# Handing Pool's loads of value quads and of reread weights to ScalarE and SP in a hybrid decoder step

## The chip, the cores and the metric

The kernel runs on one core of one Trainium2 chip. The metric is the device time of one execution in microseconds (us). The median of three runs of the kernel before is 2049.36 us (2048.97 to 2071.32). Differences under 2% (about 41 us) are called no change here.

## The reference

Two decoder layers run for a prompt group (512 tokens) and a sample group (8 tokens, one from each of 8 sequences with 4096 past tokens). Both groups share all weights. Layer 0 mixes retention with differential attention; layer 1 is a gated MLP over chunks of 128 tokens. A squared-ReLU MLP follows each layer. Cut to what matters here:

```
proj = h @ w_in                                   # layer 0, both groups
k_past = cache_k[e][page_table]; v_past = cache_v[e][page_table]   # 8 sequences x 32 pages of 128 rows
a = softmax(q1 k1) - lam * softmax(q2 k2);  do = a @ v_all          # per sequence and head
mix = concat(retention, do) @ w_out
y = y + mix;  y = y + square(relu(rms_norm(y) @ w_up)) @ w_down      # both groups
z = gelu(rms_norm(y) @ w_in_odd); u, v = split(z); ...               # layer 1
```

## The kernel before, in words

All matrix products of the prompt are made from weight chunks of 512 x 256 elements (512 KB). SP loads a chunk into one of two `raw` buffers (L637). ScalarE makes its rounded part `w_hi` (L587), and VectorE the remainder `w_lo` (L594). PE multiplies three times for each pair of parts. The chunks of the dense part of layer 0 and of the v half of layer 1 form a list of 100 places, `DENSE`, which are called steps 0 to 99 below: output projection `oe` (0 to 11), the first half of the MLP `up00` (12 to 27) and `dn00` (28 to 43), its second half `up01` (44 to 59) and `dn01` (60 to 75), and `v` (76 to 99). Each engine walks through this list in the same order, and does after its own part of a step whatever `AFTER[step]` lists for it.

Two kinds of work of the samples are listed there. `("V", i)` is the product of value quad i with the attention weights: four pages of the value cache, 1 MB, 64 quads in all, of which 30 are used up before the dense part. `("W", n)` is the product of the samples' few columns with a quad of weights (512 x 512, again 1 MB), 50 in all, in steps 47 to 89. These weights are read a second time from HBM, in other blocks than SP's chunks. There are five `W` to four steps, so eleven steps hold two. Both kinds go through the same two buffers, `vbuf0` and `vbuf1`: quad u may be loaded when quad u-2 has been used (`v_used`). PE does the product of a quad at the end of the step, after the step's chunk.

In the kernel before Pool issues all these loads (`quad_in`): at its place `("V", i)` it loads quad i+1, and at `("W", n)` quad n+1 of the weights. For a value page it reads the page's number into a register first. In the same program order Pool has other work: per macro (two chunks) of `up00` and `up01` the squares and remainders of the MLP's middle (L832, L814), sums of squares in `oe` and `dn01` (L800), the maximum over partitions for a sequence's softmax (L775), and the loads for the gating (L839 to L843). ScalarE's rounding of the middle (L1214) stands between Pool's L832 and L814.

SP's program order is, per step i: load chunk i+5, then the pages of keys listed there. What holds the load of a chunk is

```
wait(sp, lo_made, c.n - 1)                 # SP, chunk c = 41 + i: the remainder of step i+3 is made
wait(act, chunk_multiplied, c.n - 3)       # ScalarE, L587: step i+3 is rounded once step i-1 is multiplied
```

So SP's load at its step i leaves after PE has finished the chunk of step i-1, ScalarE has rounded and VectorE has made the remainder of another chunk. In `v` a macro's two chunks are multiplied together, four token tiles in turn; the first chunk counts as multiplied only with the last tile, and `AFTER` of the macro's two steps stands after the second and the fourth tile.

Of the kernel before, what the change touches and what calls it, by code (L numbers as in the profile page):

```python
# [26 lines left out]
P = 128  # L27
# [28 lines left out]
def _phases():  # L56
# [24 lines left out]
QUAD = 4  # L81
NQ, SQ = NG // QUAD, NPAGES // QUAD
K_SLOTS, Q_SLOTS = 4, 2
# [3 lines left out]
W_BLOCKS = [("oe", c, 3) for c in range(2)] + [("up", c, 2) for c in range(8)] + [("dn", c, 8) for c in range(2)] + [  # L87
    ("vv", c, 2) for c in range(6)]
W_QUADS = [(b, g) for b, (_, _, n) in enumerate(W_BLOCKS) for g in range(n)]
NW = len(W_QUADS)  # L90
# [135 lines left out]
NV1 = sum(s[0] == "V" for s in FIRST)  # L226
# [38 lines left out]
def wait(eng, sem, value):  # L265

    if isinstance(value, int) and value <= 0:
        return
    eng.wait_ge(sem, value)
# [50 lines left out]
def build(nc, x_prompt, x_sample, state_ret, cache_k, cache_v, page_table, rms_mix_g, rms_ffn_g, w_ffn_up, w_ffn_down,  # L320
# [3 lines left out]
    with ExitStack() as ctx:  # L324
# [119 lines left out]
        def kbuf(j):  # L444

            slot = j % K_SLOTS
            return kbuf_low[slot] if slot < LOW_KEYS else (kbuf_in_x if j < K1 else kbuf_on)[slot - LOW_KEYS]

        def vbuf(n):

            return vbuf_low if n % Q_SLOTS == 0 else vbuf_in_x if n < NV1 else vbuf_on
# [64 lines left out]
        def sem(name):  # L516
            return ctx.enter_context(nc.semaphore(name))
# [17 lines left out]
            sem(n) for n in ("turn_ready", "turn_read", "out_ready", "out_read", "pair_ready"))  # L535
        k_loaded = [sem(f"k_loaded{i}") for i in range(K_SLOTS)]
        v_loaded = [sem(f"v_loaded{i}") for i in range(Q_SLOTS)]
        k_scored, v_used = sem("k_scored"), sem("v_used")
        pv_zeroed, z_summed = sem("pv_zeroed"), sem("z_summed")
        k_weighed = sem("k_weighed")  # L540
# [21 lines left out]
        so_turned, so_placed, f_placed = sem("so_turned"), sem("so_placed"), sem("f_placed")  # L562
# [26 lines left out]
        def lo(dve, c):  # L589

            if isinstance(c.n, int) and c.n >= CHUNKS:
                return
            dve.wait_ge(hi_made, c.n + 1)
            dve.tensor_tensor(w_lo[:, c.slot], raw[:, c.slot % 2], w_hi[:, c.slot].bitcast(F32),  # L594
                              ALU.subtract).then_inc(lo_made, 1)
# [6 lines left out]
        def page(eng, dst, cache, n, done):  # L602

            pg = eng.value_load(ptb[0:1, n:n + 1])
            eng.dma_start(dst, cache[0][bass.ds(pg, 1)].rearrange("a t h d -> (a t) (h d)")).then_inc(done, 16)  # L605

        def osb(i):

            return osb1 if i < 1 else osb2
# [3 lines left out]
            W_OF[f"up0{h}"] = w_ffn_up[0][:, 2048 * h:2048 * h + 2048]  # L613
            W_OF[f"dn0{h}"] = w_ffn_down[0][2048 * h:2048 * h + 2048, :]
        S_OF = {"oe": (w_out_even[0], mTs), "up": (w_ffn_up[0], xgs), "dn": (w_ffn_down[0], hs), "vv": (w_in_odd[0][:, E_G:2 * E_G], xgs)}

        def quad_landed(n):

            return 16 * QUAD * (min(n, NQ) // 2 + (1 if n < NQ else 0)) + (0 if n < NQ else 16 * ((n - NQ) // 2 + 1))

        block = ctx.enter_context(nc.Block())

# [2 lines left out]
        def _(sp):  # L625
# [13 lines left out]
            def keys_in(j):  # L639
                if j < NP:  # L640
                    wait(sp, k_scored, j - K_SLOTS + 1)
                    for a in range(PER):
                        page(sp, kbuf(j)[:, a, :], cache_k, PER * j + a, k_loaded[j % K_SLOTS])

            def in_chunk(c):

                if c < 2 * N_IN:
                    chunk_in(Chunk(0, 0, 0, c), w_in_even[0], c % 2, IN_COLS[c // 2])
                elif c < PHASES["u0"][0]:
                    name, m, g = DENSE[c - 2 * N_IN]  # L650
                    chunk_in(Chunk(0, 0, 0, c), W_OF[name], g, CW * m)
# [21 lines left out]
            for m in range(N_IN + 1):  # L673
                for t in range(NT + 1):
# [12 lines left out]
                    for step in AFTER[m, t]:  # L687
# [8 lines left out]
                        if step[0] == "K" and step[1] > 0:  # L696
                            j = step[1] - 1 + K_SLOTS
# [3 lines left out]
            for j in range(K1, K1 + K_SLOTS - 1):  # L701
                if j % K_SLOTS >= LOW_KEYS:
                    keys_in(j)
            for i, key in enumerate(DENSE):
                in_chunk(2 * N_IN + AHEAD + 2 + i)
                for step in AFTER[key]:
                    if step[0] == "K":
                        keys_in(step[1] - 1 + K_SLOTS)

            def stream(name, w, per):  # L710
                c0, groups, macros = PHASES[name]

                def step(i):
                    for mm in range(per):
                        for g in range(groups):
                            chunk_in(Chunk(c0, groups * per, i, groups * mm + g), w, g, CW * per * i + CW * mm)
                repeat(sp, macros // per, step, first=1)
# [22 lines left out]
        def _(pool):  # L740
# [10 lines left out]
            pool.wait_ge(lo_made, AHEAD)  # L751
            pool.wait_ge(pt_loaded, 16)
            pool.wait_ge(xg_lo_made, KD)
            def quad_in(u):

                if u < NQ + NW:
                    wait(pool, v_used, u - Q_SLOTS + 1)
                    dst, done = vbuf(u), v_loaded[u % Q_SLOTS]
                    if u >= NV1 and u % Q_SLOTS:
                        pool.wait_ge(so_turned, 1)  # L760
                    if u < NQ:
                        for j in range(QUAD):
                            page(pool, dst[:, j, :], cache_v, QUAD * u + j, done)
                    else:
                        b, g = W_QUADS[u - NQ]
                        phase, c, _ = W_BLOCKS[b]
                        rows = S_OF[phase][0].rearrange("(g k p) n -> g p k n", k=QUAD, p=P)[g]
                        pool.dma_start(dst[:, :, :], rows[:, :, 512 * c:512 * c + 512]).then_inc(done, 16)

            def pool_steps(key):  # L770

                for kind, i, *_ in [s + (0,) for s in AFTER[key]]:
                    if kind == "soft1":
                        pool.wait_ge(row_max, i + 1)
                        pool.partition_all_reduce(mxa, mx8, P, bass.bass_isa.ReduceOp.max).then_inc(all_max, 1)  # L775
                    elif kind == "V" and i > 0:
                        quad_in(i - 1 + Q_SLOTS)
                    elif kind == "W":
                        quad_in(NQ + i - 1 + Q_SLOTS)
            for m in range(N_IN + 1):  # L780
                for t in range(NT + 1):
                    if m < LO_SWITCH and t == 1:
                        lo(pool, Chunk(0, 0, 0, 2 * m + AHEAD))
                    pool_steps((m, t))
                if m < LO_SWITCH:
                    lo(pool, Chunk(0, 0, 0, 2 * m + 1 + AHEAD))
                if 2 <= m < 2 + Q_SLOTS:
                    pool.wait_ge(x_saved, 16)
                    quad_in(m - 2)

            def add_square(e, n):

# [85 lines left out]
        def _(act):  # L878
            chain = Chain(act, act_chain)

            for row, v in ((0, rms_mix_g), (16, rms_ffn_g), (32, ln_v_g), (56, ln_v_b), (80, subln_g)):
                n = int(np.prod(v.shape)) // P
# [88 lines left out]
            def act_step(step):  # L971
                kind, i = step[0], step[1] if len(step) > 1 else None
                if kind == "ropeq":
                    n = ROPED.index(i)
# [3 lines left out]
                elif kind == "ropet":  # L978
                    n = ROPED.index(i)
# [9 lines left out]
                elif kind == "turn":  # L989
                    hh = step[2]  # L990
                    act.wait_ge(turn_ready, TURN_FILL[step] + 1)
                    dst = {0: qT, 2: kT, 6: rqT, 8: rkT}[i & ~1][:, 2 * (i % 2) + hh, :]
# [21 lines left out]
                elif kind == "softe":  # L1014
# [2 lines left out]
                    wait(act, z_summed, i - 1)  # L1017
                    act.activation(Pe[:, i % 2], Sc[:, i % 2, 0:NPAGES, :], ACT.Exp, scale=SCALE)
                    act.activation(pn[:, 8 * i:8 * i + 8], Sc[:, i % 2, NPAGES, :], ACT.Exp, scale=SCALE).then_inc(exped, 1)
                elif kind == "pvO":  # L1020
                    act.wait_ge(v_used, QUADS_TO[i])
                    if i:
# [5 lines left out]
                elif kind == "pvT" and W_BLOCKS[i - NS][0] == "vv":  # L1028
                    c = W_BLOCKS[i - NS][1]
# [81 lines left out]
                elif kind == "rB":  # L1111
                    h, n = step[1:]
# [4 lines left out]
                elif kind == "rC":  # L1117
                    h, n = step[1:]
# [108 lines left out]
            c0, _, macros = PHASES["v"]  # L1227
# [547 lines left out]
        def _(pe):  # L1775
# [67 lines left out]
            def pe_step(step):  # L1843
                kind, i = step[0], step[1] if len(step) > 1 else None
                if step in TURN_FILL:
                    wait(pe, turn_read, TURN_FILL[step])
                if kind == "turn":
                    n, hh = ROPED.index(i), step[2]
# [13 lines left out]
                elif kind == "V":  # L1862
                    s, n = i // SQ, i % SQ
                    if n == 0:
                        pe.wait_ge(exped, s + 1)
                        wait(pe, o_copied, s - 1)
                    pe.wait_ge(v_loaded[i % Q_SLOTS], quad_landed(i))
                    for j in range(QUAD):
                        at = P // QUAD * j
                        last = pe.matmul(ps[at:at + 8, PV[s % 2], :], Pe[:, s % 2, QUAD * n + j, :], vbuf(i)[:, j, :],  # L1870
# [2 lines left out]
                elif kind == "W":  # L1873
                    b, g = W_QUADS[i]
                    phase, c, groups = W_BLOCKS[b]
# [7 lines left out]
                    else:  # L1883
                        pe.wait_ge(xgs_made, 1 if phase == "up" else 2)
                    u = NQ + i
                    pe.wait_ge(v_loaded[u % Q_SLOTS], quad_landed(u))
                    for j in range(QUAD):
                        at = P // QUAD * j
                        last = pe.matmul(ps[at:at + NS, PV[b % 2], :], S_OF[phase][1][:, QUAD * g + j, :], vbuf(u)[:, j, :],  # L1889
# [2 lines left out]
                elif kind == "pvT":  # L1892
# [3 lines left out]
                    for h in range(H):  # L1896
                        last = pe.matmul(ps[:, OUT, w * h:w * h + w], osb(i)[:, P * h:P * h + P],
                                         C["fold"][:, 2 * h:2 * h + 2] if i < NS else C["fold"], start=True, stop=True)
# [74 lines left out]
                elif kind == "dA":  # L1973
# [5 lines left out]
                    for m in range(2):  # L1979
                        rows, out = slice(DH * m, DH * m + DH), ps[:, PAIR[m], 0:nk]  # L1980
# [19 lines left out]
                elif kind == "rA":  # L2000
                    h, n = step[1:]
                    c = NT * h + n
# [12 lines left out]
                elif kind == "rB":  # L2015
                    h, n = step[1:]
                    c = NT * h + n
# [115 lines left out]
            c0, _, macros = PHASES["v"]  # L2133
# [85 lines left out]
```

## Time and profile before

| | |
|---|---|
| median of 3 runs | 2049.36 us |
| time of the profiled execution | 2051.19 us |
| its span, first to last instruction | 2049.5 us |
| PE busy | 1833.3 us (89%) |
| VectorE, ScalarE, Pool busy | 1011.3, 597.1, 459.5 us |
| mean granted TensorE clock | 0.938 |
| moved by DMA | 340.31 MB, of it 120.87 MB on Pool's queue |

The profile is of one execution. A busy engine is not necessarily the bound: idle time before a group of instructions and what ended it tell more. `SPq` and `POOLq` rows are DMA issues and register work of an engine's queue. The clock is granted in two levels, full (2.4 GHz) and half (1.2 GHz).

### The profile page before, as it was taken

How to read it: one execution, taken by the hardware profiler on the slowest of the kernel's cores; microseconds unless marked ns; L12 is line 12 of the kernel's file. 1: busy time of each engine (PE TensorE's matmuls, PEld its weight loads, DVE VectorE, ACT ScalarE, POOL GpSimd, SP SyncE). 2: the span in 40 equal slices, each digit the busy share in tenths (PEclk: the TensorE clock that was granted, in tenths of full speed). 3: DMA queues.
4: the chain of work that ended last, by engine and by line, in shares of the span. 5: the costliest groups of instructions: out<-in, count | busy, mean ns of one | idle time of the engine just before them, and what ended most of it. 6: DMA issues, size and time to landing. Idle time of an engine off the chain costs nothing.

```text
span 2049.5 us, 31901 instructions
## 1 busy us (share of the span) xinstructions
PE 1833.3 (89%) x12483; PEld 1538.4 (75%) x12483; DVE 1011.3 (49%) x1344; ACT 597.1 (29%) x962; POOL 459.5 (22%) x567
## 2 busy tenths in 40 slices
PE   6858888899688878999869899989999999999998
PEld 5656546676465555677646578989999999999998
DVE  3897656887777667323213233344323443323321
ACT  5322223444323122112212133363313333212221
POOL 1321011222023444214322111003304224102400
PEclk9977778999799889999989999999999999999999
DMA  5556344798888568645556756412323232323321
GB/s 144 166 175 227 113 137 141 249 314 302 272 282 287 185 237 280 220 164 195 168 180 207 248 193 218 134 54 63 103 93 93 83 99 87 101 88 89 94 93 63
DMA packets 215634, 340.31 MB, mean 166 GB/s; under 512 B 13793, under 2 KB 150706, under 8 KB 215234
## 3 DMA queue, kind: packets, MB, share of 16 engines
q1 hardware_dynamic: 178432, 214.75, 32.3%
q0 software_dynamic: 34704, 120.87, 17.8%
q10 hardware_dynamic: 2362, 2.83, 0.4%
q8 instruction: 90, 1.47, 0.3%
q14 instruction: 46, 0.38, 0.1%
HBM read 327.19 MB, written 11.21 MB: 165 GB/s over the span
## 4 chain that ended last, share of the span: by engine, by line
PE 64%; issue 14%; DVE 8%; DMA 5%; POOL 4%; ACT 4%; POOLq 1%; ACTq 0%; SPq 0%; DVEq 0%
PE ps L2095 10%; PE ps L2093 10%; PE ps L2094 10%; PE ps L1835 5%; PE ps L1837 4%; PE ps L1836 4%; PE ps L2082 3%; PE ps L2084 3%; PE ps L2083 3%; PE ps L1870 2%; PE ps L1981 2%; PE ps L1889 2%; DMA vbuf<-in_cache_v 1%; DVE Sc L1425 1%; POOL tmp L832 1%
## 5 line engine op out<-in xcount | busy, mean ns | idle before, releaser
L594 DVE TENSOR_TENSOR w_lo<-raw,w_hi 128x1024 fp32r<-128x1024 f32 x238 | 327.5, 1381 | 482.6 <-ACT w_hi L587 481.2
L587 ACT ACTIVATE w_hi<-raw 128x1024 fp32r<-128x1024 f32 x248 | 259.2, 1053 | 410.6 <-PE ps L2095 228.1
L1835 PE MATMUL ps<-w_hi,xg_hi 128*128 128x256 f32 x960 | 290.7, 303 | 9.6 <-ACT part L916 3.2
L1836 PE MATMUL ps<-w_lo,xg_hi 128*128 128x256 f32 x960 | 279.3, 291 | 0.0
L1837 PE MATMUL ps<-w_hi,xg_lo 128*128 128x256 f32 x960 | 278.7, 290 | 0.0
L2093 PE MATMUL ps<-xg_hi,w_hi 128*128 128x260 f32 x896 | 253.2, 283 | 0.8 <-DVE vn L1761 0.8
L2095 PE MATMUL ps<-xg_hi,w_lo 128*128 128x260 f32 x896 | 253.1, 283 | 0.0
L2094 PE MATMUL ps<-xg_lo,w_hi 128*128 128x260 f32 x896 | 252.3, 282 | 0.0
L1835 PEld LDWEIGHTS ps<-w_hi,xg_hi 128*128 128x128 f32 x960 | 192.2, 200 | 49.2 <-issue 36.1
L1836 PEld LDWEIGHTS ps<-w_lo,xg_hi 128*128 128x128 f32 x960 | 192.1, 200 | 0.2
L1837 PEld LDWEIGHTS ps<-w_hi,xg_lo 128*128 128x128 f32 x960 | 191.3, 199 | 0.0
L2093 PEld LDWEIGHTS ps<-xg_hi,w_hi 128*128 128x128 f32 x896 | 168.6, 188 | 1.1 <-DVE vn L1761 1.0
L2095 PEld LDWEIGHTS ps<-xg_hi,w_lo 128*128 128x128 f32 x896 | 168.6, 188 | 0.0
L2094 PEld LDWEIGHTS ps<-xg_lo,w_hi 128*128 128x128 f32 x896 | 168.5, 188 | 0.0
L605 POOL DMA_DIRECT2D vbuf<-in_cache_v x196 | 107.2, 548 | 263.3 <-PE ps L1870 144.5
L2093 PE MATMUL ps<-h_hi,w_hi 128*128 128x260 f32 x512 | 144.6, 282 | 0.0
L2095 PE MATMUL ps<-h_hi,w_lo 128*128 128x260 f32 x512 | 144.6, 282 | 0.0
L2094 PE MATMUL ps<-h_lo,w_hi 128*128 128x260 f32 x512 | 144.5, 282 | 0.0
L832 POOL TENSOR_TENSOR tmp<-tmp 128x512 f32<-128x512 f32 (+1 forms) x64 | 65.7, 1047 | 292.3 <-DVE tmp L1700 285.3
L1422 DVE TENSOR_TENSOR kbuf<-kbuf,Qb 128x1024 f32<-128x1024 f32 x88 | 109.0, 1239 | 6.6 <-DMA kbuf<-in_cache_k 3.5
L1425 DVE TENSOR_REDUCE Sc<-kbuf 128x16 f32<-128x1024 f32 x88 | 107.4, 1220 | 3.0
L2095 PE MATMUL ps<-g_hi,w_lo 128*128 128x260 f32 x384 | 108.8, 283 | 0.0
(348 smaller groups left out, 3573.0 us busy)
## 6 DMA issues: line engine op xcount, KB each, us to landing
vbuf<-in_cache_v POOLq DMA_DIRECT2D x196, 256.0 KB, 4.6
kbuf<-in_cache_k SPq DMA_DIRECT2D x176, 256.0 KB, 4.8
raw<-in_w_ffn_up SPq DMA_DIRECT2D x64, 512.0 KB, 4.1
raw<-in_w_ffn_down SPq DMA_DIRECT2D x64, 512.0 KB, 4.1
raw<-in_w_in_odd SPq DMA_DIRECT2D x48, 512.0 KB, 3.8
raw<-in_w_in_even SPq DMA_DIRECT2D x36, 512.0 KB, 5.1
vbuf<-in_w_ffn_up POOLq DMA_DIRECT2D x16, 1024.0 KB, 6.0
vbuf<-in_w_ffn_down POOLq DMA_DIRECT2D x16, 1024.0 KB, 5.6
```

The source lines that it names most:

```text
L587: act.activation(w_hi[:, c.slot], raw[:, c.slot % 2], ACT.Copy).then_inc(hi_made, 1)
L594: dve.tensor_tensor(w_lo[:, c.slot], raw[:, c.slot % 2], w_hi[:, c.slot].bitcast(F32), ALU.subtract).then_inc(lo_made, 1)
L605: eng.dma_start(dst, cache[0][bass.ds(pg, 1)].rearrange("a t h d -> (a t) (h d)")).then_inc(done, 16)
L832: pool.tensor_tensor(tmp2[:, b, 0:w], tmp1[:, b, 0:w], tmp1[:, b, 0:w], ALU.mult).then_inc(mid_made, 1)
L1422: dve.tensor_tensor(kk[:, :, :], kk[:, :, :], Qb[:, s % 2, :].unsqueeze(1).broadcast_to([P, PER, 512]), ALU.mult).then_inc(k_weighed, 1)
L1425: dve.tensor_reduce(Sc[:, s % 2, g:g + PER, :], kk[:, :, :].rearrange("p a (b c) -> p a b c", c=DH), AXX, ALU.add).then_inc(k_scored, 1)
L1835: pe.matmul(out, xh, wh, start=kk == 0, stop=False, skip_group_check=True)
L1836: pe.matmul(out, xh, wl, start=False, stop=False, skip_group_check=True)
L1837: mm = pe.matmul(out, xl, wh, start=False, stop=kk == KD - 1, skip_group_check=True)
L2093: pe.matmul(out, wh, xh, start=kk == 0, stop=False, skip_group_check=True)
L2094: pe.matmul(out, wh, xl, start=False, stop=False, skip_group_check=True)
L2095: mm_ = pe.matmul(out, wl, xh, start=False, stop=kk == KC * groups - 1, skip_group_check=True)
```

## The change

The loads of reread weights go from Pool to SP: after its chunk of a step, SP issues at `("V", 63)` quad 0 and at `("W", n)` quad n+1. Value quads 0 to 30 and the even ones after that stay with Pool; the 17 odd ones from 31 to 63 are issued by ScalarE, at the same places of the list, on a semaphore of their own. Products, buffers and the list itself stay. In the diff `sample_weights_in` is SP's and the last `values_in(act, ...)` ScalarE's.

```
+        def by_pool(u):
+            return u <= NV1 or u < NQ and u % Q_SLOTS == 0
+        def quad_landed(u):
+            if by_pool(u):
+                return v_loaded[u % Q_SLOTS], 16 * QUAD * (u // Q_SLOTS + 1)
+            return v_loaded_on[u % Q_SLOTS], sum(16 * (QUAD if n < NQ else 1) for n in range(u, 0, -Q_SLOTS) if not by_pool(n))
+        def values_in(eng, u):
+            if u < NQ:
+                wait(eng, v_used, u - Q_SLOTS + 1)
+                if u >= NV1 and u % Q_SLOTS:
+                    eng.wait_ge(so_turned, 1)
+                for j in range(QUAD):
+                    page(eng, vbuf(u)[:, j, :], cache_v, QUAD * u + j, quad_landed(u)[0])
...
+            def sample_weights_in(n):
+                u = NQ + n
+                sp.wait_ge(v_used, u - Q_SLOTS + 1)
...
+                sp.dma_start(vbuf(u)[:, :, :], rows[:, :, 512 * c:512 * c + 512]).then_inc(quad_landed(u)[0], 16)
             for i, key in enumerate(DENSE):
                 in_chunk(2 * N_IN + AHEAD + 2 + i)
                 for step in AFTER[key]:
                     if step[0] == "K":
                         keys_in(step[1] - 1 + K_SLOTS)
+                    if step == ("V", NQ - 1):
+                        sample_weights_in(0)
+                    if step[0] == "W" and step[1] + 1 < NW:
+                        sample_weights_in(step[1] + 1)
...
-                    elif kind == "V" and i > 0:
-                        quad_in(i - 1 + Q_SLOTS)
-                    elif kind == "W":
-                        quad_in(NQ + i - 1 + Q_SLOTS)
+                    elif kind == "V" and i > 0 and by_pool(i - 1 + Q_SLOTS):
+                        values_in(pool, i - 1 + Q_SLOTS)
...
+                elif kind == "V" and i > 0 and not by_pool(i - 1 + Q_SLOTS):
+                    values_in(act, i - 1 + Q_SLOTS)
...
-                    pe.wait_ge(v_loaded[u % Q_SLOTS], quad_landed(u))
+                    pe.wait_ge(*quad_landed(u))
```

What the change moves shows at two places. The first is Pool in macros 0 to 4 of `v` (`vbuf_71` is `vbuf0`, `vbuf_115` is `vbuf1`): before, the weights' loads stand there one behind the other, and nothing but `v_used` holds them (`so_turned` was reached long before).

```order
885 L768 DMA vbuf_71<-in_w_ffn_down 128x4x512 [waits v_used]
886 L768 DMA vbuf_115<-in_w_ffn_down 128x4x512 [waits so_turned,v_used]
887 L768 DMA vbuf_71<-in_w_in_odd 128x4x512 [waits v_used]
888 L768 DMA vbuf_115<-in_w_in_odd 128x4x512 [waits so_turned,v_used]
889 L768 DMA vbuf_71<-in_w_in_odd 128x4x512 [waits v_used]
890 L768 DMA vbuf_115<-in_w_in_odd 128x4x512 [waits so_turned,v_used]
```

The same loads now stand on SP, from quad 37 of the weights (first row) to quad 42 (last but one):

```order
912 L726 DMA vbuf_115<-in_w_ffn_down 128x4x512 [waits v_used]
913 L726 DMA vbuf_71<-in_w_in_odd 128x4x512 [waits v_used]
914 L652 DMA raw<-in_w_in_odd 128x4x256 [waits lo_made] x3
915 L726 DMA vbuf_115<-in_w_in_odd 128x4x512 [waits v_used]
916 L726 DMA vbuf_71<-in_w_in_odd 128x4x512 [waits v_used]
917 L652 DMA raw<-in_w_in_odd 128x4x256 [waits lo_made]
918 L726 DMA vbuf_115<-in_w_in_odd 128x4x512 [waits v_used]
919 L652 DMA raw<-in_w_in_odd 128x4x256 [waits lo_made]
920 L726 DMA vbuf_71<-in_w_in_odd 128x4x512 [waits v_used]
```

Quad 39 (row 915) moved from a place behind quad 38 alone to one behind three chunks that wait for `lo_made`.

The second place is Pool at the end of `oe`, before: quad 39 of the values (rows 500 to 511) stands behind the maximum over partitions.

```order
498 L775 ISA
499 L775 ISA tiny<-tiny 128x8 [waits row_max]
500 L604 TENSOR_LOAD ptb [waits so_turned,v_used]
501 L605 ISA
502 L605 DMA vbuf_115<-in_cache_v 128x512
```

The same quad now stands on ScalarE, behind the rounding of a chunk:

```order
456 L588 ACTIVATE w_hi<-raw 128x1024 [waits raw_loaded0,chunk_multiplied]
457 L588 ACTIVATE w_hi<-raw 128x1024 [waits raw_loaded1,chunk_multiplied]
458 L605 TENSOR_LOAD ptb [waits so_turned,v_used]
459 L606 ISA
460 L606 DMA vbuf_115<-in_cache_v 128x512
```

It no longer follows row 499; the next `w_hi` of ScalarE now follows its four pages.

## Rows read from the trace of the kernel before

**Rows 1.** Groups by line, PE's sample products: busy, mean ns | idle before, releaser.
```profile
L1870 PE MATMUL ps<-vbuf,Pe 128*8 128x512 f32 x392 | 56.0, 646 | 37.0 <-DMA vbuf<-in_cache_v 37.0
L1889 PE MATMUL ps<-vbuf,xgs 128*8 128x512 f32 x224 | 32.4, 656 | 26.2 <-DMA vbuf<-in_w_ffn_up 25.7 <-DMA vbuf<-in_w_in_odd 0.5
L1889 PE MATMUL ps<-vbuf,hs 128*8 128x512 f32 x128 | 16.5, 594 | 7.6 <-DMA vbuf<-in_w_ffn_down 7.6
```

**Rows 2.** Timeline of PE, value quads 39, 42, 47: start, duration, [idle before <-releaser].
```profile
660.76 1.89 PE L1870 MATMUL ps<-vbuf,Pe 128*8 128x512 f32 x8 [6.21 <-DMA vbuf<-in_cache_v]
...
701.90 1.90 PE L1870 MATMUL ps<-vbuf,Pe 128*8 128x512 f32 x8 [6.34 <-DMA vbuf<-in_cache_v]
...
759.72 1.90 PE L1870 MATMUL ps<-vbuf,Pe 128*8 128x512 f32 x8 [13.52 <-DMA vbuf<-in_cache_v]
```

**Rows 3.** Timeline of Pool around the loads of value quads 39, 42 and 47.
```profile
652.68 0.40 POOL L775 PARTITION_ALL_REDUCE tiny<-tiny  x1 [10.61 <-issue]
...
670.30 2.66 POOL L800 TENSOR_TENSOR sqsum<-sqsum,sq 128x512 f32<-128x512 f32 x2 [8.68 <-issue]
...
751.43 1.83 POOL L605 DMA_DIRECT2D vbuf<-in_cache_v  x3
```

**Rows 4.** Timeline of ScalarE, the two chunks rounded before value quad 47.
```profile
749.58 1.99 ACT L587 ACTIVATE w_hi<-raw 128x1024 fp32r<-128x1024 f32 x2
```

**Rows 5.** Timeline of SP, issue of four pages of keys.
```profile
717.31 3.07 SPq L605 DMA_DIRECT2D kbuf<-in_cache_k  x4
```

**Rows 6.** Timeline of PE, reread weights: quads 7, 15, 32, 36+37, 38+39, 48+49.
```profile
992.44 1.89 PE L1889 MATMUL ps<-vbuf,xgs 128*8 128x512 f32 x8 [5.41 <-DMA vbuf<-in_w_ffn_up]
...
1066.39 1.90 PE L1889 MATMUL ps<-vbuf,xgs 128*8 128x512 f32 x8 [15.17 <-DMA vbuf<-in_w_ffn_up]
...
1176.18 1.04 PE L1889 MATMUL ps<-vbuf,hs 128*8 128x512 f32 x8 [2.92 <-DMA vbuf<-in_w_ffn_down]
...
1212.29 1.90 PE L1889 MATMUL ps<-vbuf,hs 128*8 128x512 f32 x16
...
1234.30 1.90 PE L1889 MATMUL ps<-vbuf,xgs 128*8 128x512 f32 x16
...
1295.43 2.09 PE L1889 MATMUL ps<-vbuf,xgs 128*8 128x512 f32 x16
```

**Rows 7.** Timeline of SP, loads of chunks at steps 54, 74, 77+78, 81, 89.
```profile
987.47 0.37 SPq L637 DMA_DIRECT2D raw<-in_w_ffn_up  x1
...
1167.20 0.37 SPq L637 DMA_DIRECT2D raw<-in_w_in_odd  x1
...
1207.42 2.70 SPq L637 DMA_DIRECT2D raw<-in_w_in_odd  x2
...
1237.11 0.37 SPq L637 DMA_DIRECT2D raw<-in_w_in_odd  x1
...
1297.46 0.37 SPq L637 DMA_DIRECT2D raw<-in_w_in_odd  x1
```

**Rows 8.** DMA issues: queue, count, KB each, median us from issue to landing.
```profile
vbuf<-in_cache_v POOLq DMA_DIRECT2D x196, 256.0 KB, 4.6
kbuf<-in_cache_k SPq DMA_DIRECT2D x176, 256.0 KB, 4.8
raw<-in_w_ffn_up SPq DMA_DIRECT2D x64, 512.0 KB, 4.1
...
vbuf<-in_w_ffn_up POOLq DMA_DIRECT2D x16, 1024.0 KB, 6.0
vbuf<-in_w_ffn_down POOLq DMA_DIRECT2D x16, 1024.0 KB, 5.6
...
xT<-x_kept SPq DMA_DIRECT2D x1, 2080.0 KB, 7.9
```

**Rows 9.** Waits: who waited for whom, us in total, times, longest.
```profile
POOL vbuf L768 <- issue: 187.6, 37, 7.3
```

**Rows 10.** Windows: stretch, length, busy of PE to POOL, PEclk, DMA share, GB/s.
```profile
760.00:770.00 10.00, 10.00 (x41) 5.89 (x34) 6.80 (x7) 3.74 (x5) 7.21 (x9) 0.75 0.82 296
```

More of the change, by code:

```diff
@@ L537, in build @@
         v_loaded = [sem(f"v_loaded{i}") for i in range(Q_SLOTS)]
+        v_loaded_on = [sem(f"v_loaded_on{i}") for i in range(Q_SLOTS)]
         k_scored, v_used = sem("k_scored"), sem("v_used")
@@ L615, in build @@
         S_OF = {"oe": (w_out_even[0], mTs), "up": (w_ffn_up[0], xgs), "dn": (w_ffn_down[0], hs), "vv": (w_in_odd[0][:, E_G:2 * E_G], xgs)}
-        def quad_landed(n):
-            return 16 * QUAD * (min(n, NQ) // 2 + (1 if n < NQ else 0)) + (0 if n < NQ else 16 * ((n - NQ) // 2 + 1))
         block = ctx.enter_context(nc.Block())
@@ L703, in _ @@
                     keys_in(j)
+            def sample_weights_in(n):
+                u = NQ + n
+                sp.wait_ge(v_used, u - Q_SLOTS + 1)
+                b, g = W_QUADS[n]
+                phase, c, _ = W_BLOCKS[b]
+                rows = S_OF[phase][0].rearrange("(g k p) n -> g p k n", k=QUAD, p=P)[g]
+                sp.dma_start(vbuf(u)[:, :, :], rows[:, :, 512 * c:512 * c + 512]).then_inc(quad_landed(u)[0], 16)
             for i, key in enumerate(DENSE):
@@ L753, in _ @@
             pool.wait_ge(xg_lo_made, KD)
[L754 to L768, printed above, removed]
             def pool_steps(key):
@@ L788, in _ @@
                     pool.wait_ge(x_saved, 16)
-                    quad_in(m - 2)
+                    values_in(pool, m - 2)
             def add_square(e, n):
@@ L1866, in pe_step @@
                         wait(pe, o_copied, s - 1)
-                    pe.wait_ge(v_loaded[i % Q_SLOTS], quad_landed(i))
+                    pe.wait_ge(*quad_landed(i))
                     for j in range(QUAD):
```

## Prediction

> **What bounds the kernel now.** Read the groups by line first. PE is busy for 89% of the span, so only what makes PE wait or slows its clock can move the end. Two of PE's groups are touched: the samples' value products (L1870), which wait 37.0 us in all for value loads, and their products with reread weights (L1889), which wait 26.2 + 7.6 = 33.8 us [rows 1]. That is the stock from which the change could gain: about 71 us, 3.5% of the span. PE's timeline then tells where the stock lies. Three value quads hold 26 of the 37 us: 39 with 6.2, 42 with 6.3 and 47 with 13.5 us [rows 2]. Of the weights, quad 15 alone holds 15.2 us; the rest is a few us at the second product of a double step, such as 5.4 at quad 7 and 2.9 at quad 32, all of it in `up01` and `dn01` [rows 6]. In `v` PE goes through both products of a step without a wait: 36 and 37, 38 and 39, 48 and 49 each stand as one row of 16 matmuls [rows 6].
>
> Each long wait has a second price. In the ten us behind the wait of 13.5 us the granted clock is 0.75 [rows 10], part of the time at the half level of 1.2 GHz: 2.5 us lost. The eight products behind waits of 5.4 and 15.2 us take 1.89 us instead of 1.04, those behind 2.9 us don't [rows 6]. I charge 2.5 us for a wait of five us or more, 1.5 for the one of 3.9 at quad 12, nothing below three.
>
> **The weights on SP.** What holds such a load changes. On Pool it was `v_used` and Pool's queue; on SP it also stands behind the chunk load of its step, which leaves only when a remainder is made, that is after PE has finished the chunk before. For a double step (quads n, n+1) the load of n+1 stands behind this step's chunk, and PE wants it at the end of this step. So I take the time of SP's chunk load, add what the load takes, and compare with the time at which PE came to the product.
>
> The price of a 1 MB load on SP isn't in the trace. The nearest rows are Pool's own 1 MB loads, 6.0 and 5.6 us [rows 8]; I take 5.8, plus 0.9 for the two issues (0.37 for the chunk [rows 7], about as much for the quad): the quad lands 6.7 us after the chunk load began. The ends are SP's 512 KB chunk, 4.1 us, and SP's 2080 KB load, 7.9 us [rows 8]; 5.8 is nearest because size and pattern are the same and only the issuer differs.
>
> The Trainium skill ("DMA: Bandwidth & Descriptors", "Issuing engine by pattern") calls issue from SP or ScalarE generally faster than from Pool, with a first byte after about 0.6 instead of 1 us. By it each of 14 late loads would be 0.4 us earlier, some 6 us less in the sum (an estimate); this trace doesn't show it, as SP's 256 KB pages land after 4.8 us and Pool's after 4.6 [rows 8].
>
> *up01 and dn01*, seven doubles. Quad 7: chunk load at 987.5 [rows 7] + 6.7 = 994.2; PE was ready at 992.4 − 5.4 = 987.0 [rows 6]: a wait of 7.1 us, against 5.4. Quad 32: 1167.2 + 6.7 = 1173.9 against 1173.3: 0.6, against 2.9. Worked out alike the seven give 3.1 (quad 2), 7.1, 5.8, 3.0, 0.7, 1.4 and 0.6 = 21.7 us, against 17.7 now. Quad 15's wait of 15.2 goes: it comes from the gating's loads ahead of it on Pool (L839 to L843), which SP doesn't have; so does 0.8 of quad 28. Sum 21.7 − 33.7 = **−12.0**.
>
> *v*, four doubles and the singles around them. Here the load of the chunk at a macro's second step leaves only when the macro's last tile is multiplied, which is when PE turns to the samples. Quad 39: 1237.1 + 6.7 = 1243.8, wanted at 1234.3 + 1.0 = 1235.3 [rows 6, 7]: 8.5 us of wait where there was none. Quad 44 has the same place (8.5); quad 49: 1297.5 + 6.7 − 1296.4 = 7.8. Quads 36 and 37 stand behind the two chunk loads at 1207.4 and 1209.8: 1214.1 against 1212.3, then 1216.5 against 1215.1, so 1.8 and 1.4. Quads 42 and 47, each 1.9. Sum 31.8, against 0.5 now: **+31.3**.
>
> *Clock.* Slowed stretches now: behind quads 7, 15 (2.5 each) and 12 (1.5) = 6.5; then: behind 7, 12, 39, 44, 49 = 12.5. **+6**.
>
> SP's wait for `v_used` is satisfied no later than the next chunk's own condition, so I cost nothing for chunks behind it; they are loaded five steps ahead. If that cover were gone, ScalarE's rounding would be late next.
>
> **The values.** Quad 39's load stood on Pool behind the maximum over partitions, with 10.6 us of idle time charged to "issue" before it and 8.7 more before the sums behind it [rows 3]. On ScalarE it leaves at once, so its 6.2 us go; but PE next waits for Pool's sums of squares (L800), which come some 4 to 5 us earlier because Pool has shed this quad's issue: of 6.2 I count **−5**, without a clock gain. Quad 47 leaves Pool at 751.4 [rows 3]; on ScalarE it stands behind the rounding of a chunk, done at about 750.6 [rows 4]: **−0.8**. Quad 42, with the even 34, 36, 38, 50 and 52, stays on Pool. Its DMA now meets that of ScalarE's quad beside it: two loads share the engines, where 1 MB more costs (7.9 − 4.1) / 1568 KB = 2.5 us [rows 8]; I charge 1.5 each at 42 and 52: **+3**. ScalarE issues 17 quads at the 3.07 us that SP needs for four pages [rows 5], 52 us in all; ScalarE works three steps ahead of PE, which hides one issue per step, so 0; without that cover the next `w_hi`, and PE behind it, would be up to 3 us late, 17 times. Pool's saved 2.3 us or so per quad free idle Pool time, 0.
>
> **The sum:** −12.0 + 31.3 + 6 − 2.8 = +22.5 us. The sum is against the profiled execution (2051.2), which is 1.8 above the median of the runs; on the median, 2049.4 + 22.5 = **2072 us**. With loads of 4.1 us instead of 5.8 the fourteen waits shrink and two fall under the clock's price: about +1, 2051. With 7.9 us: about +51, 2100.
>
> **The rivals.**
>
> *A, the forecast:* late weights in `v` cost more than quad 15 gives: 2055 to 2090. Chance 0.58.
>
> *B, the values win.* If the "issue" time before Pool's work [rows 3, 9] is its queue being full, half the pages on another engine could empty it: nearly all 37.0 us at L1870 [rows 1] and four slowed stretches of 2.3 go, 46 us; less 25 for the weights: about 2028. For it: Pool's quad loads wait 187.6 us for "issue", 37 times [rows 9]; against it, the largest waits, 42 and 47, stay behind the same macro's work. Chance 0.11; 2% faster (2008) needs the weights to come free as well.
>
> *C, slower.* One mechanism: 1 MB through SP's queue lands later than Pool's, behind the 512 KB chunk issued just ahead of it on the same queue. At 7.2 us or more, 1.4 later on 14 waits, 20 us more: 2092, and 2100 at the far end of 7.9 [rows 8]. It decides from 7.2 us. For it: the chunk is still moving when the quad starts, and 1 MB costs 2.5 us by the slope above; against it, Pool's 5.8 already held such neighbours. Chance 0.18.
>
> *D, no difference.* The loads are the same bytes on the same DMA engines; if the issuer only spends its own time, PE's waits stay about what they are: 2049. This is against the order of instructions, by which a load in `v` can't leave before the chunk load, and against the 187.6 us that Pool's loads waited at issue [rows 9]. Chance 0.09.
> The Trainium skill says so in "DMA: Bandwidth & Descriptors", "Issuing engines are not separate DMA queues": spreading issues over engines parallelises only the issuing, usually a small gain. This trace disagrees as far as rows 9 go: here the issuing engine's queue held loads back.
>
> The remaining 0.04 is for what I haven't seen, such as ScalarE losing its cover.
>
> **Range and chances.** A, D and half of C lie between 2045 and 2097, about 0.8. Faster by over 2% (2008): 0.03; slower by over 2% (2090): C and the tail of A, 0.19; within: 0.78. Two per cent, 41 us, is about what a measurement of this kernel can tell from no change, given runs from 2049.0 to 2071.3.
>
> **What the profile would show.** Right: PE idle about 8 us before the second product of quads 39, 44 and 49, none at quad 15, and quad 39 of the values without a wait; DMA issues of 1 MB on SP near 5.8 us; waits at value quads 42, 47 and 52 much as before. Wrong: SP's quads landing before PE's second product in `v`; waits at 42 and 47 gone (B); or new idle time before L587 or before PE's first product of a chunk, which would mean that ScalarE's or SP's lead doesn't hide the new issues.

## The result, and the profile after

The changed kernel takes 2097.03 us (median of 4 runs, 2096.78 to 2102.31). The kernel before, in runs on the same chips, takes 2055.72 (2048.97 to 2071.32). The ratio is 1.0196, 95% interval 1.0129 to 1.0264: slower by 27 to 54 us. That it is slower is clear of the scatter; whether by more than the 2% line is not, since the interval lies on both sides of it. The profiled execution took 2102.31 us with a span of 2100.6, 51.1 longer than the profiled one of before. PE is busy for 1845.7 us instead of 1833.3 with the same 12483 instructions, and the mean granted clock is 0.928 instead of 0.938.

The groups by line of the changed kernel, PE's sample products and its products with Pool's sums (busy, mean ns | idle before, releaser; to be held against [rows 1]):

```profile
L1882 PE MATMUL ps<-vbuf,Pe 128*8 128x512 f32 x392 | 55.3, 638 | 41.0 <-DMA vbuf<-in_cache_v 41.0
L1901 PE MATMUL ps<-vbuf,xgs 128*8 128x512 f32 x224 | 35.0, 702 | 45.0 <-DMA vbuf<-in_w_in_odd 27.1 <-DMA vbuf<-in_w_ffn_up 17.9
L1901 PE MATMUL ps<-vbuf,hs 128*8 128x512 f32 x128 | 18.7, 659 | 11.8 <-DMA vbuf<-in_w_ffn_down 11.8
L1901 PE MATMUL ps<-vbuf,mTs 128*8 128x512 f32 x48 | 7.1, 668 | 6.7 <-DMA vbuf<-in_w_out_even 6.7
L2133 PE MATMUL ps<-sqsum,ones 128*128 128x512 f32 x4 | 3.2, 888 | 6.8 <-POOL sqsum L810 6.8
```

Before, the last two of these groups read:

```profile
L1889 PE MATMUL ps<-vbuf,mTs 128*8 128x512 f32 x48 | 6.3, 594 | 0.3 <-DMA vbuf<-in_w_out_even 0.3
L2121 PE MATMUL ps<-sqsum,ones 128*128 128x512 f32 x4 | 3.2, 886 | 3.1 <-POOL sqsum L800 3.1
```

Waits for reread weights rose from 34.1 to 63.5 us; the largest part, 27.1, is in `v`, where there was 0.5. Value waits rose from 37.0 to 41.0, and the wait for Pool's sums of squares from 3.1 to 6.8. With 12.4 us more of PE's busy time that is 49.5 of the 51.1 us.

This sum runs over the whole span, and part of the span is not touched by the change. The next two views cut both executions at the same products of PE: at the ends of value quad 29 (all loads up to here are as before), value quad 63, reread quad 35 (`up01` and `dn01`) and reread quad 49 (`v`). The columns are the stretch, its length, PE's busy time, the granted clock, the share of the DMA engines and GB/s. Before:

```profile
0.00:529.40 529.40, 429.03 (x2806) 0.87 0.60 197
529.40:903.10 373.70, 314.45 (x1481) 0.91 0.73 251
903.10:1205.70 302.60, 264.29 (x1313) 0.94 0.58 190
1205.70:1297.50 91.80, 91.31 (x763) 1.00 0.66 218
1297.50:2049.50 752.00, 734.19 (x6131) 0.99 0.28 86
```

After:

```profile
0.00:523.40 523.40, 421.50 (x2806) 0.88 0.61 198
523.40:907.30 383.90, 316.83 (x1477) 0.90 0.73 245
907.30:1213.30 306.00, 269.55 (x1317) 0.93 0.54 185
1213.30:1345.70 132.40, 100.75 (x767) 0.87 0.46 163
1345.70:2100.60 754.90, 737.13 (x6128) 0.99 0.28 85
```

The first stretch is 6.0 us shorter after; over the eleven profiled kernels, none of which changes anything there, it takes 517.6 to 529.4 us, so this is scatter. Behind it the changed execution is 57 us longer: 10.2 in the values, 3.4 in `up01` and `dn01`, 40.6 in `v`, 2.9 in the rest. PE's busy time behind the first stretch rose by some 20 us, not 12.4; 9.4 of them are in `v`, where the granted clock fell from 1.00 to 0.87.

PE's timeline of the changed kernel (start, duration, what ended the idle time): value quads 39, 47 and 50, then reread quads 15, 32, 37, 39, 44 and 49.

```profile
660.24 1.05 PE L1882 MATMUL ps<-vbuf,Pe 128*8 128x512 f32 x8
...
759.61 1.89 PE L1882 MATMUL ps<-vbuf,Pe 128*8 128x512 f32 x8 [12.04 <-DMA vbuf<-in_cache_v]
...
800.33 1.90 PE L1882 MATMUL ps<-vbuf,Pe 128*8 128x512 f32 x8 [12.53 <-DMA vbuf<-in_cache_v]
...
1068.90 1.04 PE L1901 MATMUL ps<-vbuf,xgs 128*8 128x512 f32 x8 [0.56 <-DMA vbuf<-in_w_ffn_up]
...
1179.84 1.89 PE L1901 MATMUL ps<-vbuf,hs 128*8 128x512 f32 x8 [2.69 <-DMA vbuf<-in_w_ffn_down]
...
1225.65 1.89 PE L1901 MATMUL ps<-vbuf,hs 128*8 128x512 f32 x8 [3.07 <-DMA vbuf<-in_w_ffn_down]
...
1258.31 1.89 PE L1901 MATMUL ps<-vbuf,xgs 128*8 128x512 f32 x8 [8.36 <-DMA vbuf<-in_w_in_odd]
...
1302.21 1.90 PE L1901 MATMUL ps<-vbuf,xgs 128*8 128x512 f32 x8 [8.09 <-DMA vbuf<-in_w_in_odd]
...
1343.80 1.89 PE L1901 MATMUL ps<-vbuf,xgs 128*8 128x512 f32 x8 [7.51 <-DMA vbuf<-in_w_in_odd]
```

Value quad 39 no longer waits, quad 47 waits 12.0 us in place of 13.5 [rows 2], and quad 50, an even one that stayed on Pool, waits 12.5; before, quad 50 waited 1.4 and quad 52 5.9, which is gone. Reread quad 15 has lost its 15.2 us, and quads 39, 44 and 49 have waits of about 8 us where there were none [rows 6].

SP's timeline around reread quad 39's load shows the mechanism: the chunk load of step 81, and behind it quad 39 (with quad 40).

```profile
1251.71 0.37 SPq L652 DMA_DIRECT2D raw<-in_w_in_odd  x1
1252.12 1.06 SPq L726 DMA_DIRECT2D vbuf<-in_w_in_odd  x2
```

PE had finished the macro and came to quad 39 at about 1250; the product starts 6.6 us after the chunk load.

### The profile page after: what moved, and what is told of

Read it like the earlier page. It is cut to its first block, busy times and chain, and to the rows that moved or that the text cites. A ratio compares the mean times of both kernels' runs of the same rounds, so it can differ in the third digit from the quotient of the medians.

```text
span 2100.6 us, 31879 instructions
## 1 busy us (share of the span) xinstructions
PE 1845.7 (88%) x12483; PEld 1546.8 (74%) x12483; DVE 1011.5 (48%) x1344; ACT 596.7 (28%) x962; POOL 384.8 (18%) x449
## 4 chain that ended last, share of the span: by engine, by line
PE 61%; issue 15%; DVE 8%; DMA 7%; ACT 4%; POOL 3%; POOLq 1%; SPq 0%; ACTq 0%; DVEq 0%
PE ps L2107 10%; PE ps L2105 10%; PE ps L2106 10%; PE ps L1847 4%; PE ps L1849 4%; PE ps L1848 4%; PE ps L2094 3%; PE ps L2096 3%; PE ps L2095 2%; PE ps L1882 2%; PE ps L1993 2%; DMA vbuf<-in_w_ffn_down 1%; DMA vbuf<-in_w_in_odd 1%; POOL tmp L842 1%; PE ps L1901 1%
## 5 line engine op out<-in xcount | busy, mean ns | idle before, releaser
L1847 PE MATMUL ps<-w_hi,xg_hi 128*128 128x256 f32 x960 | 294.3, 307 | 9.1 <-DVE xg_lo L1682 3.1
L1847 PEld LDWEIGHTS ps<-w_hi,xg_hi 128*128 128x128 f32 x960 | 195.4, 204 | 52.8 <-issue 41.8
L606 POOL DMA_DIRECT2D vbuf<-in_cache_v x128 | 70.3, 550 | 248.6 <-PE ps L1882 124.5
```

Source lines behind the costliest of these rows:

```text
L1847: pe.matmul(out, xh, wh, start=kk == 0, stop=False, skip_group_check=True)
```

## The experiments

The theory after the result: the weights on SP cost the time, because they stand behind chunk loads that have no lead over PE. The rivals: ScalarE's value loads cost it, or SP's queue is slower for 1 MB. Each ratio is to runs of the kernel before on the same chip; those spread from 2042 to 2069 us over all the experiments, and the intervals allow for that. Medians of different experiments come from different chips; a difference of a few us between two of them is not sharp.

**One half of the change at a time.** All values on Pool, weights on SP (`e1`), by one line of `by_pool`:

```
-            return u <= NV1 or u < NQ and u % Q_SLOTS == 0
+            return u < NQ
```

> All values stay on Pool, only the reread weights go to SP. Theory (the weights cost the time, because SP's load of a weight quad leaves behind a chunk load that leaves only when PE is done with the chunk before): waits at L1901 of about 60 us in place of 34, 8 us each at quads 39, 44 and 49, none at 15; 2075 to 2090 us. Rival (ScalarE's value loads cost it, by colliding with Pool's): 2045 to 2055 us.

Measured: 2084.79 us, ratio 1.0162 (1.0135 to 1.0188). The waits at L1901 add up to 60.5 us (by the weights that are read: 6.0 for `oe`'s, 17.4 for `up01`'s, 8.9 for `dn01`'s, 28.3 for `v`'s), 8.5, 8.0 and 7.9 of them at quads 39, 44 and 49. The theory's figures hold.

The other half (`e2`): weights on Pool as before, odd values on ScalarE:

```
+            return u <= NV1 or u >= NQ or u % Q_SLOTS == 0
...
+                    elif kind == "W" and i + 1 < NW:
+                        sample_weights_in(i + 1)
```

> The reread weights stay on Pool, the odd values go to ScalarE. Theory: quad 39's wait is gone, quads 42 and 47 wait as before, a few us more at the even quads; reread weights wait 34 us as before; 2045 to 2058 us. Rival (ScalarE's loads cost the time): over 2070 us.

Measured: 2061.55 us, ratio 1.0043 (1.0019 to 1.0067): slower by 7 us by the medians and 9 by the ratio, under the 2% line but clear of the scatter, and a little above the times expected. Quad 39's wait is gone, but the value waits are 40.5 us in all: 5.0 at quad 36 and 11.6 at quad 50, and PE waits 9.0 us for Pool's sums of squares. The reread weights wait 37.7 us, a few more than expected. The two ratios multiply to 1.0206; the whole change has 1.0196. So the weights make some four fifths of the loss, the values the rest.

**The place behind the chunk load** (`e3`): the changed kernel, but with the first reread quad of a step issued ahead of the step's chunk.

```
+                first = next((step for step in AFTER[key] if step[0] == "W" and step[1] + 1 < NW), None)
+                if first:
+                    sample_weights_in(first[1] + 1)
                 in_chunk(2 * N_IN + AHEAD + 2 + i)
...
-                    if step[0] == "W" and step[1] + 1 < NW:
+                    if step[0] == "W" and step[1] + 1 < NW and step != first:
                         sample_weights_in(step[1] + 1)
```

> The changed kernel, but SP issues the first reread quad of a step ahead of the step's chunk load instead of behind it. Theory (what is late is the place behind the chunk load): waits at quads 39, 44 and 49 fall from 8 us each to under 2, the 1 MB loads land after about 5.8 us instead of 7.2, and the time comes to 2045 to 2062 us. Rival (SP's queue is simply slower for 1 MB than Pool's, wherever the load stands): they still take about 7 us to land, and the time stays over 2080 us.

Measured: 2018.17 us, ratio 0.9823 (0.9787 to 0.9859), better than expected. Its PE groups:

```profile
L1904 PE MATMUL ps<-vbuf,xgs 128*8 128x512 f32 x224 | 28.3, 594 | 3.4 <-DMA vbuf<-in_w_ffn_up 1.8 <-DMA vbuf<-in_w_in_odd 1.6
L1904 PE MATMUL ps<-vbuf,hs 128*8 128x512 f32 x128 | 16.5, 594 | 1.9 <-DMA vbuf<-in_w_ffn_down 1.9
L1904 PE MATMUL ps<-vbuf,mTs 128*8 128x512 f32 x48 | 6.3, 594 | 1.8 <-DMA vbuf<-in_w_out_even 1.8
```

Of 63.5 us 7.1 are left, and the mean of one product is 594 ns throughout, with no slowed ones. The same loads on the same queue, two lines earlier, turn a loss into a gain of 36 us for the kernel as a whole. This is the experiment that shows the cause. Cut into the same stretches, `e3` takes 263.4 us in `up01` and `dn01` (302.6 before, 306.0 in the changed kernel) and 93.9 us in `v` (91.8 and 132.4). So the new order takes away the loss in `v`; the gain over the kernel before is made in `up01` and `dn01`, for a reason that `e4` shows. By the Trainium skill ("DMA: Bandwidth & Descriptors", "Issuing engines are not separate DMA queues") issuing from several engines saves only the time of issuing, usually a small gain. Here the place in the issuer's order was worth 79 us by the medians (77 by the ratios) between two kernels that use the same engines.

**Where the loss is made** (`e7`): values on Pool, reread quads 0 to 37 on SP behind the chunks as in the change, 38 to 49 on Pool.

```
+            return u < NQ or u >= NQ + 38
...
+                    if step[0] == "W" and step[1] + 1 < 38:
+                        weights_in(sp, step[1] + 1)
...
+                    elif kind == "W" and 38 <= i + 1 < NW:
+                        weights_in(pool, i + 1)
```

> Values on Pool, reread weights 0 to 37 on SP behind the chunk loads as in the change, 38 to 49 on Pool again. Theory (nearly all of the loss is made in v, by quads 39, 44 and 49 and their clock): about 31 us less than the run with all weights on SP, 2050 to 2058 us, no wait over 2 us from quad 39 on. Rival (the loss is made in oe, up01 and dn01, where 1 MB loads take 7 us): 2070 us or more.

Measured: 2051.04 us, ratio 0.9973 (0.9948 to 0.9998), and no wait over 1.5 us from quad 39 on. The 12 quads of `v` cost the 34 us between this run and `e1` (39 by the ratios); the 38 before them are worth nothing or a few us of gain on SP.

**Quad 15** (`e4`): the kernel before, with Pool's gating loads moved behind its work in `dn01`.

```
-                if h:
-                    gate_in()
                 between(f"dn0{h}", 2 if h else None)
+            gate_in()
```

> The kernel before, with Pool's five loads for the gating moved behind its work in dn01. Theory (quad 15's wait of 15.2 us is these loads' time on Pool): that wait goes, with 2.5 us of slowed clock: about 2032 us. Rival (the wait comes from something else on Pool at the turn from up01 to dn01): quad 15 waits 10 us or more still, 2049 us.

Measured: 2052.17 us, ratio 0.9991 (0.9966 to 1.0017): no change. The wait at quad 15 is gone, as expected, and yet nothing is won: the waits for weights add up to 33.1 us, against 34.1 before. 5.2 of it stand at quad 35, where the gating's loads now are, those at quads 17 to 32 rose from 8.9 to 14.3 and those behind quad 35 from 0.5 to 4.0; quads 7 and 12 wait 9.5, against 9.3. Pool's timeline of this kernel, loads of weights with nothing else between them:

```profile
1151.32 0.76 POOL L768 DMA_DIRECT2D vbuf<-in_w_ffn_down  x1 [7.10 <-issue]
1157.49 0.76 POOL L768 DMA_DIRECT2D vbuf<-in_w_ffn_down  x1 [5.42 <-issue]
1163.14 0.75 POOL L768 DMA_DIRECT2D vbuf<-in_w_ffn_down  x1 [4.89 <-issue]
1169.36 0.76 POOL L768 DMA_DIRECT2D vbuf<-in_w_ffn_down  x1 [5.46 <-issue]
```

They leave 5.7 to 6.2 us apart, each held by "issue". What holds them shows in the landings: these four landed 5.9, 5.3, 5.9 and 5.3 us after they left, and each next one leaves 0.3 us after the one before it has landed. In the kernel before this holds for 37 of the 49 pairs of consecutive reread loads on Pool, and none leaves earlier, though `v_used` would let it. PE uses five quads in four steps of about 6.7 us and one more product, some 5.6 us a quad. So in `up01` and `dn01` Pool's own pace sets the time: a wait taken away at one quad comes back at the next ones. That explains the miss; it was read from the trace and not tried by itself. On SP, which issues two 1 MB loads in 1.06 us (rows above), the pace is not there: in the changed kernel 29 of the 49 leave before the one ahead has landed, and in `e3` the waits did go.

**Values back to Pool with the weights ahead** (`e5`): `e3` with the line of `e1`.

> As the run with the reread weights ahead of the chunk load, but with all values back on Pool. If the two halves of the change add up, as the two runs of one half each suggest (30.6 and 7.3 us), this is some 7 us faster than that run: about 2011 us, with value waits as in the kernel before (34 to 37 us). Rival (ScalarE's values cost nothing, and the 7 us are scatter): 2018 us.

Measured: 2009.08 us, ratio 0.9765 (0.9725 to 0.9806), 9 us under `e3`, though the intervals of the two ratios overlap. The traces agree on the size better: from value quad 29 to value quad 63 the split costs 7.5 us here (375.3 against 382.8 in `e3`), and some 12 both with the late weights (372.3 in `e1`, 383.9 in the changed kernel) and with the weights on Pool (373.7 before, 386.0 in `e2`). So the split of the values costs time with and without the late weights.

**All dense quads on SP** (`e6`): `by_pool` is `u <= NV1`, nothing is issued by ScalarE, and the first quad of a step, values or weights, goes ahead of the chunk.

```
+                quads = [u for u in quads if NV1 < u < NQ + NW]
+                for u in quads[:1]:
+                    reread_in(u)
                 in_chunk(2 * N_IN + AHEAD + 2 + i)
...
+                for u in quads[1:]:
+                    reread_in(u)
```

> All value quads of the dense part go to SP as well, and the first reread quad of a step, values or weights, is issued ahead of the step's chunk load. Theory (the value waits come from the place behind Pool's other work and from Pool's pauses between pages): the 35 to 40 us at the value products fall below 12 and the time to 1970 to 1995 us. Rival (the value waits are DMA time, with 270 GB/s moved in these stretches): they stay over 30 us, or the chunk loads behind them become late and PE waits at its first product of a chunk; 2010 us or more.

Measured: **1979.59 us**, ratio 0.9636 (0.9589 to 0.9683), faster than both kernels by 3.6% and 5.6%. Value waits fell to 19.3 us, not below 12 as expected, and 12.1 of these stand at quad 48; quad 47 (the first row), where the long wait was before, has 0.5:

```profile
717.28 1.04 PE L1889 MATMUL ps<-vbuf,Pe 128*8 128x512 f32 x8 [0.53 <-DMA vbuf<-in_cache_v]
...
736.20 1.89 PE L1889 MATMUL ps<-vbuf,Pe 128*8 128x512 f32 x8 [12.10 <-DMA vbuf<-in_cache_v]
```

Pool's timeline of `e6` ahead of that wait shows the maximum over partitions and the squares behind it; SP's, below it, shows a chunk load, which waits for a remainder, and quad 48 behind it.

```profile
710.64 0.40 POOL L796 PARTITION_ALL_REDUCE tiny<-tiny  x1 [10.39 <-DVE tiny L1569]
719.33 2.04 POOL L851 TENSOR_TENSOR tmp<-tmp 128x512 f32<-128x512 f32 x2 [8.29 <-issue]
```

```profile
725.00 0.39 SPq L652 DMA_DIRECT2D raw<-in_w_ffn_up  x1
...
729.45 3.15 SPq L606 DMA_DIRECT2D vbuf<-in_cache_v  x4
```

**The maximum behind the squares** (`e8`): `e6` with Pool's squares of a macro ahead of the maximum.

```
-                                pool_steps((name, 2 * i + mm, g))
+                                pool_steps((name, 2 * i + mm, g), ("V",))
                         for b in range(2):
                             make(b, 4 * i + 2 * mm + b)
+                        if name in L0:
+                            for g in range(2):
+                                pool_steps((name, 2 * i + mm, g), ("soft1",))
```

> As the run with all dense quads on SP, but in up00 and up01 Pool does the squares of a macro ahead of the maximum over partitions listed there. Theory (the 12 us at quad 47, which stay whoever issues the load, come from this maximum: Pool's squares stand 8.3 us behind it, ScalarE's rounding of the middle waits for them, the next chunk's rounding for that, and SP's load of quad 47 for the chunk's remainder): the wait at quad 47 falls below 6 us and the time by 6 to 10 us, to 1970 to 1974 us. Rival (the wait comes from the DMA engines or the load's own place): 10 us or more stay, and the time stays at 1980 us.

The wait that this calls quad 47's is quad 48's in `e6`, as shown above.

Measured: 1981.40 us, ratio 0.9629 (0.9602 to 0.9656), the same as `e6`. Its PE and Pool timelines:

```profile
735.29 1.90 PE L1892 MATMUL ps<-vbuf,Pe 128*8 128x512 f32 x8 [4.37 <-DMA vbuf<-in_cache_v]
...
769.75 1.90 PE L1892 MATMUL ps<-vbuf,Pe 128*8 128x512 f32 x8 [4.46 <-DMA vbuf<-in_cache_v]
```

```profile
719.22 1.04 POOL L854 TENSOR_TENSOR tmp<-tmp 128x512 f32<-128x512 f32 x1
726.99 0.39 POOL L796 PARTITION_ALL_REDUCE tiny<-tiny  x1 [6.73 <-issue]
735.20 2.52 POOL L836 TENSOR_TENSOR hA_lo<-tmp,hA_hi 128x512 fp32r<-128x512 f32 x2 [7.81 <-issue]
```

The wait at quad 48 fell from 12.1 to 4.4 us, so most of it came from the maximum's place ahead of the squares; in the other kernels, where quad 47 waits, this was not tried. The median did not follow. Between 720.3 and 735.2 Pool's only row is the maximum, of 0.4 us, with idle time charged to "issue" before and behind it; it now stands ahead of the next remainders and squares, and the wait at quad 51 rose from 2.4 to 4.5. From value quad 29 to value quad 63 the profiled execution is 2.7 us shorter than that of `e6` (346.1 against 348.8), and the untouched stretch before it 6.6 us longer, so the runs cannot tell whether a few us were won.

**All dense values on ScalarE** (`e9`): `e3` with `by_pool` as `u <= NV1`.

> As the run with reread weights ahead of the chunk load, but all dense value quads on ScalarE and none on Pool. Theory (the worse waits at the even quads 36 and 50 come from Pool's pauses between its pages, 7.5 us inside quad 50): no wait over 3 us at quads 36, 38 and 50, quads 42 and 47 still wait, 1985 to 2005 us. Rival (ScalarE's 33 issues of 3 us hold up its rounding): PE waits at first products of chunks, 2015 us or more.

Measured: 1987.93 us, ratio 0.9659 (0.9633 to 0.9686). No wait at quads 36, 38 and 50; 3.7 at quad 42, 9.8 at quad 47. PE's first products of chunks (L1850) wait 7.3 us in all, against 9.6 at that line before: ScalarE's 33 issues are hidden. So it was not ScalarE's issuing that cost time in the change, but the even quads left on Pool beside it.

## Why the prediction was right in direction and short in size

- **The term of `v` held.** 31.8 us were forecast and 31.7 found: 8.36, 8.09 and 7.51 at quads 39, 44 and 49 (8.5, 8.5, 7.8 forecast), 1.49, 3.07, 1.40 and 1.73 at quads 36, 37, 42 and 47. Here a load took what was assumed: quad 39's product starts 6.6 us after the chunk load, against 6.7. `e3` and `e7` show that this mechanism is the loss.
- **The term of `up01` and `dn01` was mis-sized**, by 10 us: 31.8 us of waits in `up01` and `dn01` (the weights of `oe` are reread there too) instead of 21.7. The step that failed is the price of 5.8 us for 1 MB on SP. The DMA issues of the changed kernel:

```profile
vbuf<-in_w_ffn_up SPq DMA_DIRECT2D x16, 1024.0 KB, 7.2
vbuf<-in_w_ffn_down SPq DMA_DIRECT2D x16, 1024.0 KB, 6.6
...
vbuf<-in_w_in_odd SPq DMA_DIRECT2D x12, 1024.0 KB, 6.1
vbuf<-in_w_out_even SPq DMA_DIRECT2D x6, 1024.0 KB, 6.9
```

  Single loads show where the price failed (in us, from issue to landing):

| reread quad | the load took | PE waits | forecast wait |
|---|---|---|---|
| 7, 12, 27 | 6.1, 5.6, 6.1 | 7.1, 5.2, 1.4 | 7.1, 5.8, 1.4 |
| 17, 22, 32 | 9.1, 8.6, 8.2 | 5.1, 3.1, 2.7 | 3.0, 0.7, 0.6 |
| 1 | 8.2 | 5.1 | 3.1, put at quad 2 |
| 5 | 7.9 | 1.5 | none |

  The second product of the first double step is quad 1's, so the 3.1 us that the prediction puts at quad 2 belong to it. Rival C's price was real for the lower three rows, but not by the mechanism that C names: quads 7, 12, 39, 44 and 49 stand just as close behind a chunk load and took 5.6 to 6.1 us. At quads 17, 22 and 32 the 1 MB quad before had not landed when the load left, at those five it had. That may explain three of the five slow loads but was not tried; what slowed quads 1 and 5 is open. Quad 15's 15.2 us did go, but `e4` shows that this alone is worth nothing on Pool. In all, `up01` and `dn01` became 3.4 us longer, where −12 of waits was forecast.
- **The values' term had the wrong sign.** −2.8 us was forecast, and this stretch became 10.2 us longer. Quad 39's wait went, and PE then waited for Pool's sums, as forecast; but these came no earlier (they start at 671.2 us, before at 670.3 [rows 3]; 6.8 us of wait instead of 3.1), and the even quads 36 and 50 became worse. The charge of 1.5 us each for quads that share the engines with ScalarE's missed where it would fall and how much: Pool's timeline of the changed kernel, the pages of quad 50.

```profile
784.77 1.11 POOL L606 DMA_DIRECT2D vbuf<-in_cache_v  x2
793.37 0.54 POOL L606 DMA_DIRECT2D vbuf<-in_cache_v  x1 [7.49 <-issue]
```

  Two pages leave, then Pool stands still for 7.5 us in the middle of a quad. With the values off Pool (`e6`, `e9`) the waits at 36 and 50 are gone, so the pause or its place on Pool made them. What Pool pauses for is open. VectorE ran eight instructions without a gap from 784.0 to 794.2. The Trainium skill ("SBUF — State Buffer", "Terms") says that VectorE and GpSimd share a port pair, held for a whole instruction, and that the loser is fully blocked. But in the kernel before Pool issued a page at 785.54 while L1422, with two inputs, ran from 784.99 to 786.20. So the rule alone does not explain these rows, and no run here separates it.
- **The clock's term was too small**: 6 us was forecast, and PE's busy time behind value quad 29 rose by 20 us at the lower clock. In `v` it rose by 9.4, where three slowed stretches of 2.5 each were charged; `up01` and `dn01` have 5.3 of the rest, the values 2.4, what stands behind `v` 2.9. There were more waits, and the bound of three us was wrong: the products behind 2.69 and 3.07 us (quads 32 and 37) ran at 1.89 us for eight, the half level, where those behind 2.92 before had run in 1.04 [rows 6].
- **Rival B** is refuted for this change: half the pages on another engine did not empty the waits, 41.0 us remain. Its idea was half right: with all dense pages off Pool 19.3 us (`e6`) and 17.4 us (`e9`) are left of 37.0. The 187.6 us that it leans on [rows 9] are those of the 1 MB weight loads, one at a time (`e4`), not of pages. **Rival D** is refuted by the ratio of 1.0196.
- **What was costed at nothing** held: ScalarE's issues are hidden (`e9`), and PE's wait before the first product of a chunk (L1847) is 9.1 us in the changed kernel, against 9.6.

The direction and the main mechanism were right, and they were not luck. The size was a little over half of what came: +22.5 us were forecast, and the medians differ by 41. The median, 2097.03, lies at the upper edge of the 2045 to 2097 that A, D and half of C cover, above A's own 2055 to 2090 and close to C's 2092, so that the time alone does not tell A from C; the waits in `v` do. That the range held is in part luck: the three misses, of `up01` and `dn01`, of the values and of the clock, all went the same way, and only the half of C that was counted in reaches so far. The profiled execution was 5 us longer than the median.

## What to carry to other kernels

When a load moves to another engine, look first at what that engine waits for just ahead of it: a queue that feeds the bottleneck engine "just in time" has no lead to give, and a load behind its wait is late by the whole transfer. Put the load that is wanted next ahead of the one that is wanted five steps later, and the move can turn from 2% slower to 2% faster. And before a wait is counted as gain, look whether the loads behind it run at a pace of their own, each waiting for the one before to land: there the time comes back at the next load.

## What the runs showed of the hardware beyond that

- Pool had one 1 MB load in flight at a time: the next left 0.3 us after the one before had landed (37 of 49 in the kernel before, none earlier), 5.7 to 6.2 us apart in the rows of `e4`. SP issued two within 1.06 us.
- Around the maximum over partitions of a 128x8 tile, 0.4 us in its row, Pool did nothing else for some 15 us (720.3 to 735.2 in `e8`); the idle time on both sides is charged to "issue".
- Behind a wait of about 3 us PE ran eight products at the full level or at the half, even in one execution: in the changed kernel 1.05 us behind 2.92 us (value quad 38) and 1.89 us behind 2.69 us (reread quad 32).
